# The first stage of a two-block transformer kernel: modulation as one half and two quarters, four projection chunks held in PSUM, and memory slabs moved into the half

## The chip, the cores and the metric

The kernel runs on one core of one Trainium2 chip. The metric is the device time of one execution in microseconds (us). The engines are TensorE (PE in the profile; PEld is its weight load), VectorE (DVE), ScalarE (ACT), GpSimd (POOL, unused here) and SyncE (SP), which issues nearly all transfers.

## The reference, cut to what matters

Two transformer blocks run one after the other over 256 tokens of width 2048. Only the start of the first block is touched, and a part of the second that depends on an input of its own:

```python
ada = jax.nn.silu(c) @ w_ada[l] + b_ada[l]            # 2048 -> 6 x 2048
shift_m, scale_m, gate_m, shift_f, scale_f, gate_f = split(ada)
h = rms_norm(x, g_pre_mix[l]) * (1.0 + scale_m) + shift_m
z = h @ w_in[l]                                       # 2048 -> 3920
...
k, v = jnp.split(mem_n @ wkv, 2, axis=-1)             # second block: 256 memory rows, 2048 -> 2 x 512
```

`z` is then split into the inputs of a latent attention (MLA) and a gated linear attention (GLA). All weights are float32.

## The kernel before, in words

**Slabs.** Every weight passes through four raw buffers of 128 x 2048 float32 (`raw`, 1 MiB each), which SP fills in one order written out by hand. A slab is 1024 KB, or less where a chunk is narrower. SP may issue slab n when slab n-4 is done (`slab_done`, L434). There are two kinds:

- A *linear* slab feeds matmuls. ScalarE rounds it into `wh` (`hi`, L631), VectorE makes the rest `wl = raw - wh` (`lo`, L1964), which frees the raw buffer. TensorE then runs, for two row blocks and four k-tiles, three matmuls each, hi x hi, hi x lo and lo x hi (L1283 to L1285): 24 matmuls a slab (`slab_mm`). There are two `wh`/`wl` buffers; `hi` of a slab waits until the slab two before it is used (`slab_used`).
- A *modulation* slab (w_ada) is multiplied by silu(c) and added up by VectorE alone, in ACC, JUNK or ACC2, which frees the buffer.

Every engine walks the slabs in the same order, with its own program. `skip` and `st.next(False)` pass a slab that another engine handles.

**First stage.** x is normalised, turned by TensorE and copied to XS by ScalarE. Then ScalarE takes the statistics of the memory and the sines of the rotary angles, and only after those walks on through its slabs. The shift and scale of the modulation are made in four quarters of 512 columns. A quarter is 8 slabs (`ada_part`: 4 row tiles x 512 columns for shift or scale). VectorE adds a slab up in four 128x512 steps (L2165; the first ones L2157). TensorE sums over partitions with small matmuls (`mod_parts`, L1356, 32 instructions), VectorE makes shift and gain (`mod_part`), then ScalarE and VectorE make four k-tiles of the modulated h (`h_hi`, L732; `h_gained`, L2190; `h_lo`). Such a quarter of h lets one quarter of the rows of w_in be used. `ZCH` lists nine chunks of columns of w_in with widths 400, 512, 512, 320, 320, 416, 416, 512, 512; a chunk takes four slabs, one for each quarter of h, and two PSUM banks (one per row block). Three chunks (ZK = 3) are held in banks 0 to 5, and after each quarter of h three w_in slabs are used. The eight slabs of w_xkv (memory keys and values, banks 6 and 7) lie between them, and most of the next quarter's modulation slabs (`AHEAD`) are placed ahead of the w_in slabs. The order is 8 modulation slabs with 1 memory slab; then for q = 0, 1, 2: memory, 2 modulation, w_in, 1 modulation, w_in, 2 modulation, w_in, 1 modulation, memory, 2 modulation; then memory and three w_in. That makes 52 slabs: 32 modulation, 8 memory, 12 w_in.

**Loop.** The other six chunks follow, 24 slabs (ZR = 24), with GLA's work between them (`a_turn`, `gate`, `cumulated`, ... on TensorE, the gate functions on ScalarE, the scans on VectorE). One full row tile of 8 KB per partition of the gate modulation goes with most slabs (`ADA_SHIFT`: 16 of them, into ACC), and 7 of the next (`ADA_NEXT`, into ACC2) with the last ones. ACC must have been zeroed (`acc_zero`, L2004) before SP loads a bias row into it (L444); SP does so in order, after the second slab of the loop. `ADA_FIRST` = 7 is how many rows of the second sum are made in the loop. The rest come later: two with w_uk and w_uv, one before and six within MLA's head loop (VectorE, L1985), where the number is KT - ADA_FIRST - 3.

## Time and profile before

| | |
|---|---|
| median of 3 runs | 2699.1 us (2698.87 to 2699.74) |
| the profiled execution | 2705.51 us, span 2703.7 us |
| TensorE busy | 2602.7 us (96% of the span) |
| VectorE busy | 1668.6 us (62%) |
| ScalarE busy | 1151.0 us (43%) |
| mean granted TensorE clock | 0.981 |
| read from HBM | 561.69 MB, 210 GB/s over the span |

A busy TensorE is not one at its peak: ends of matmuls are modelled, so a pipelined matmul shows 390 ns where the next starts 230 ns later. A wait in brackets behind an instruction is idle time of its engine, with what ended it. "x24" is a count of merged instructions. Idle time of an engine that is not the bottleneck costs nothing by itself.

### The profile page before, as it was taken

The numbers are of one execution on the slowest core, as the hardware profiler recorded it, in microseconds if no ns is written. First come the engines' busy times: TensorE is split into PE (matmuls) and PEld (weight loads), VectorE is DVE, ScalarE is ACT, GpSimd is POOL, SyncE is SP. The second block draws the span as 40 slices with busy tenths as digits, with TensorE's granted clock in tenths as the row PEclk, the third lists the DMA queues.
The fourth block names the chain that finished last, engine by engine and source line by source line (L and its number), as shares of the span: only waits on it lengthen the run. The fifth ranks groups of instructions, "written<-read, shape, count | busy, mean of one in ns | idle before, by whom it ended". The sixth has DMA issues, their size and how long they took to land.

```text
span 2703.7 us, 30651 instructions
## 1 busy us (share of the span) xinstructions
PE 2602.7 (96%) x12149; PEld 2158.3 (80%) x12149; DVE 1668.6 (62%) x1700; ACT 1151.0 (43%) x1217; POOL 0.2 (0%) x4
## 2 busy tenths in 40 slices
PE   5899999899999999999999999999899999999998
PEld 4778778788887888887988888787688888888886
DVE  7878788856665555557446665655555555555556
ACT  5244544443333333335445455444653333333333
POOL 0000000000000000000000000000000000000000
PEclk8999999899999999999999999999999999999999
...
GB/s 330 360 262 324 330 220 324 243 252 253 254 253 209 190 192 191 186 186 157 239 172 140 150 147 152 171 202 153 143 187 186 186 189 191 193 188 186 186 187 139
DMA packets 268139, 568.20 MB, mean 210 GB/s; under 512 B 9857, under 2 KB 46591, under 8 KB 258704
## 3 DMA queue, kind: packets, MB, share of 16 engines
...
q8 instruction: 61, 1.00, 0.2%
q14 instruction: 28, 0.23, 0.0%
HBM read 561.69 MB, written 5.24 MB: 210 GB/s over the span
## 4 chain that ended last, share of the span: by engine, by line
PE 80%; DVE 5%; ACT 3%; issue 2%; DMA 1%; DVEq 0%; ACTq 0%
PE bank L1283 25%; PE bank L1285 24%; PE bank L1284 24%; ACT wh L631 2%; DVE wl L1964 1%; DVE ROWB L1964 1%; DVE ACC L1985 1%; DMA raw<-in_w_out 1%; PE bank L1252 1%; PE bank L1816 1%; PE bank L1645 1%; PE bank L1764 1%; PE bank L1799 0%; DVE X L2118 0%; DMA raw<-in_w_uq 0%
## 5 line engine op out<-in xcount | busy, mean ns | idle before, releaser
L1964 DVE TENSOR_TENSOR wl<-raw,wh 128x2048 fp32r<-128x2048 f32 (+4 forms) x434 | 975.6, 2248 | 875.6 <-ACT wh L631 875.1
L631 ACT ACTIVATE wh<-raw 128x2048 fp32r<-128x2048 f32 (+4 forms) x434 | 816.4, 1881 | 1317.9 <-PE bank L1285 1209.8
L1283 PE MATMUL bank<-wh,XTh 128*128 128x512 f32 (+4 forms) x2680 | 1044.5, 390 | 21.9 <-DVE wl L1964 15.9
L1285 PE MATMUL bank<-wh,XTl 128*128 128x512 f32 (+4 forms) x2680 | 1032.5, 385 | 0.0
L1284 PE MATMUL bank<-wl,XTh 128*128 128x512 f32 (+4 forms) x2680 | 1031.6, 385 | 0.0
L1283 PEld LDWEIGHTS bank<-wh,XTh 128*128 128x128 f32 x2680 | 506.1, 189 | 126.8 <-issue 18.3
L1285 PEld LDWEIGHTS bank<-wh,XTl 128*128 128x128 f32 x2680 | 505.5, 189 | 94.4
L1284 PEld LDWEIGHTS bank<-wl,XTh 128*128 128x128 f32 x2680 | 506.2, 189 | 91.1 <-issue 0.5
L1283 PE MATMUL bank<-wh,HTh 128*128 128x512 f32 x640 | 251.1, 392 | 3.0 <-DVE ROWB L1964 3.0
L1285 PE MATMUL bank<-wh,HTl 128*128 128x512 f32 x640 | 249.2, 389 | 0.0
L1284 PE MATMUL bank<-wl,HTh 128*128 128x512 f32 x640 | 249.1, 389 | 0.0
L1283 PEld LDWEIGHTS bank<-wh,HTh 128*128 128x128 f32 x640 | 120.1, 188 | 34.7 <-issue 10.5
L1285 PEld LDWEIGHTS bank<-wh,HTl 128*128 128x128 f32 x640 | 120.1, 188 | 25.1
L1284 PEld LDWEIGHTS bank<-wl,HTh 128*128 128x128 f32 x640 | 120.2, 188 | 24.4
L1964 DVE TENSOR_TENSOR ROWB<-ROWB,bank 128x512 f32<-128x512 f32 x176 | 112.7, 682 | 8.8 <-PE bank L1285 7.2
L1985 DVE SCALAR_TENSOR_TENSOR ACC<-raw,cT,ACC 128x2048 f32<-128x2048 f32 x46 | 108.0, 2349 | 2.5
L1981 DVE SCALAR_TENSOR_TENSOR ACC<-raw,cT,ACC 128x2048 f32<-128x2048 f32 x16 | 37.6, 2350 | 1.8 <-DVE wl L1964 1.2
L2165 DVE SCALAR_TENSOR_TENSOR JUNK<-raw,cT,JUNK 128x512 f32<-128x512 f32 x56 | 38.1, 747 | 0.0
L2165 DVE SCALAR_TENSOR_TENSOR ACC<-raw,cT,ACC 128x512 f32<-128x512 f32 x56 | 37.9, 745 | 0.0
L624 ACT ACTIVATE XTh<-bank,vT 128x256 fp32r<-128x256 f32 x54 | 21.5, 474 | 28.8 <-PE bank L1252 21.7
L1061 ACT ACTIVATE Z<-bank,nstat 128x512 f32<-128x512 f32 (+1 forms) x24 | 16.2, 674 | 41.3 <-PE bank L1285 41.2
L1283 PE MATMUL bank<-wh,MTh 128*128 128x512 f32 x64 | 28.6, 446 | 2.8 <-DVE wl L1964 1.1
...
## 6 DMA issues: line engine op xcount, KB each, us to landing
raw<-in_w_ada SPq DMA_DIRECT2D x96, 1024.0 KB, 6.3
raw<-in_w_in SPq DMA_DIRECT2D x48, 1024.0 KB, 5.2
raw<-in_w_ffn_gate SPq DMA_DIRECT2D x44, 1024.0 KB, 5.2
raw<-in_w_ffn_up SPq DMA_DIRECT2D x44, 1024.0 KB, 5.2
raw<-in_w_ffn_down SPq DMA_DIRECT2D x44, 1024.0 KB, 5.0
raw<-in_w_gate SPq DMA_DIRECT2D x44, 1024.0 KB, 5.2
raw<-in_w_up SPq DMA_DIRECT2D x44, 1024.0 KB, 5.1
raw<-in_w_down SPq DMA_DIRECT2D x44, 1024.0 KB, 5.0
```

What stands on the lines that cost most here:

```text
L631: act.activation(wh[:, st.lin % 2, 0:width], raw[:, st.raw % 4, 0:width], ACT.Copy).then_inc(hi_made, 1)
L1252: mm = pe.transpose(PB[turn_bank(name, b)][:, SEQ * k + P * r:SEQ * k + P * r + P], src(r, 2 * b + k), ident)
L1283: pe.matmul(out_, hi_t[:, k, rows], w[0][:, q, :], start=first and q == 0, stop=False)
L1284: pe.matmul(out_, hi_t[:, k, rows], w[1][:, q, :], start=False, stop=False)
L1285: mm = pe.matmul(out_, lo_t[:, k, rows], w[0][:, q, :], start=False, stop=last and q == n - 1)
L1645: mm = pe.transpose(PB[4 + b][:, SEQ * q + P * r:SEQ * q + P * r + P], HROW[:, r, P * (2 * b + q):P * (2 * b + q) + P], ident)
L1764: pe.matmul(PB[2 + u % 2][:, 0:2 * nk].rearrange("p (b n) -> p b n", b=2), QT(i, par, r), KT2(g, nk), start=True, stop=True).then_inc(S("n ...
L1816: pe.matmul(PB[7][:, HD * b:HD * b + HD], pT[:, u % 2, P * blk_:P * blk_ + P], Z2[:, k, c0:c0 + HD], start=k == 0, stop=k == r)
L1964: return dve.tensor_tensor(out_, a, b, op)
L1981: ins = dve.scalar_tensor_tensor(acc[:, :], w, cT[:, bass.ds(k0 + k, 1)], acc[:, :], ALU.mult, ALU.add)
L1985: ins = dve.scalar_tensor_tensor(acc[:, :], w, cT[:, k:k + 1], acc[:, :], ALU.mult, ALU.add)
L2165: ins = dve.scalar_tensor_tensor(part, w, c, part, ALU.mult, ALU.add)
```

## The change

- The modulation of the first 1024 columns is made at once (`ada_half`: 16 slabs, one row tile each, 1024 columns of shift and 1024 of scale, one 128x2048 step into ACC), the rest in two quarters (`ada_quarter`: 8 slabs each, two row tiles, two transfers of 512 KB on one semaphore, two 128x1024 steps into JUNK or ACC).
- Three stages with an order made by `interleaved`: (0) two modulation slabs, then memory slab and two modulation slabs by turns, the eighth memory slab last; (1) w_in slab and one quarter slab by turns, for four chunks (ZK = 4) and the two quarters of h that the half gives, the last w_in slab after the last two quarter slabs; (2) w_in slab and two quarter slabs by turns, the fourth w_in slab last, behind four.
- The fourth use of the four chunks is moved into the loop as its first four slabs (`z_slab`). The loop still has 24 slabs: these four, and five chunks.
- Memory keys are summed in banks 4 and 5, values in 6 and 7; the key transposes use banks 2 and 3. All eight banks then hold the four chunks. Banks of the later chunks, of the gate and of the cq and ckv turns are swapped to suit, and TensorE waits for the last chunk's copies ahead of w_uq.
- GLA's steps are placed one slab later in the loop, the statistics of the latents one group earlier. `acc_zero` comes after the last quarter of h. ADA_FIRST is 6 instead of 7.

The diff, cut to its core. `mod_part` becomes `mod_made`, with the same three steps on 8 columns for the half:

```diff
@@ -83,14 +83,33 @@
 FN_ADA = KT // 4
-ZK = 3
-ZR = 4 * (ZN - ZK)
-AHEAD = ((0, 1), (2,), (3, 4))
-ADA_SHIFT = (1, 2, 3) + tuple(range(5, 18))
-ADA_NEXT = {ZR - 6: 1, ZR - 5: 2, ZR - 4: 1, ZR - 3: 1, ZR - 2: 1, ZR - 1: 1}
+ZK = 4
+ZR = 4 * (ZN - ZK) + 4
+ADA_SHIFT = (2, 3) + tuple(range(5, 19))
+ADA_NEXT = {ZR - 5: 2, ZR - 4: 1, ZR - 3: 1, ZR - 2: 1, ZR - 1: 1}
 next_row = {n: sum(ADA_NEXT[m] for m in ADA_NEXT if m < n) for n in ADA_NEXT}
 ADA_FIRST = sum(ADA_NEXT.values())
 XKV = [(i // 4, i % 4) for i in range(8)]
+def interleaved(slabs, rows, first, each):
+    steps = [("ada", k) for k in range(first)]
+    k = first
+    for i in range(slabs - 1):
+        steps.append(("slab", i))
+        steps += [("ada", k + m) for m in range(each)]
+        k += each
+    return steps + [("ada", m) for m in range(k, rows)] + [("slab", slabs - 1)]
+STAGES = [interleaved(8, 16, 2, 2), interleaved(8, 8, 0, 1), interleaved(4, 8, 0, 2)]
+MOD_READY = (4, 4, 6, 8)
+def z_slab(n):
+    return (n, 3) if n < 4 else (3 + n // 4, n % 4)
 BUCKETS, MAXD = 32, 2048
 REL_W = SEQ + P
...
+    def landed(self, transfers=1):
+        return self.plus(16 * (self.raw // 4 + self.more[self.raw % 4] + transfers), 4 * self.praw)
+    def next(self, linear=True, transfers=1):
+        self.more[self.raw % 4] += transfers - 1
...
-        return 2 + (TURN0[name] + b) % 2
+        return (TURN0[name] + b) % 2
...
+        mod_at = PB[1][:, 496:512]
         def z_banks(c):
-            return (2 * c, 2 * c + 1) if c < ZK else (2 * (c % 2), 2 * (c % 2) + 1)
+            return (2 * c, 2 * c + 1) if c < ZK else (2 - 2 * (c % 2), 3 - 2 * (c % 2))
...
-            def ada_part(v, q, s):
-                slab(W["w_ada"][:, 4 * s:4 * s + 4, v * D + 512 * q:v * D + 512 * q + 512], (4, 512), False)
+            def ada_half(k):
+                rows = W["w_ada"][:, k, 0:2 * D].rearrange("p (v n) -> p v n", v=2)
+                slab(rows[:, :, 0:1024], (2, 1024), False)
+            def ada_quarter(q, k):
+                rows = [W["w_ada"][:, 2 * k + t, 0:2 * D].rearrange("p (v n) -> p v n", v=2)[:, :, 512 * q:512 * q + 512]
+                        for t in range(2)]
+                sp.wait_ge(slab_done, st.raws(-3))
+                for t in range(2):
+                    dst = raw[:, st.raw % 4, 1024 * t:1024 * t + 1024].rearrange("p (v n) -> p v n", v=2)
+                    sp.dma_start(dst, rows[t]).then_inc(landed[st.raw % 4], 16)
+                st.next(False, 2)
...
-            for v in range(2):
-                for s in range(4):
-                    ada_part(v, 0, s)
-                if v == 0:
-                    xkv(0)
-            for q in range(4):
-                xkv(2 * q + 1)
-                for c in range(ZK):
-                    if q < 3:
-                        for s in AHEAD[c]:
-                            ada_part(s // 4, q + 1, s % 4)
-                    cols("w_in", q, *ZCH[c])
-                if q < 3:
-                    ada_part(1, q + 1, 1)
-                    xkv(2 * q + 2)
-                    for s in range(2, 4):
-                        ada_part(1, q + 1, s)
-                if q == 1:
+            for what, i in STAGES[0]:
+                ada_half(i) if what == "ada" else xkv(i)
+            for what, i in STAGES[1]:
+                ada_quarter(2, i) if what == "ada" else cols("w_in", i % 2, *ZCH[i // 2])
+                if (what, i) == ("slab", 3):
                     sp.wait_ge(S("rel_row"), 1)
                     sp.wait_ge(S("angle"), 1)
...
+            for what, i in STAGES[2]:
+                ada_quarter(3, i) if what == "ada" else cols("w_in", 2, *ZCH[i])
...
-                cols("w_in", n % 4, *ZCH[ZK + n // 4])
+                cols("w_in", z_slab(n)[1], *ZCH[z_slab(n)[0]])
...
+            for what, i in STAGES[0][3:]:
+                if what == "ada":
+                    skip()
+                    continue
                 hi()
...
+            h_hi(0)
+            for what, i in STAGES[1]:
+                if what == "ada":
+                    st.next(False, 2)
+                    continue
+                hi(4 * ZCH[i // 2][1])
+                if i == 0:
+                    h_hi(1)
+                if i == 1:
+                    act.wait_ge(slab_used, 8)
+                    for r in range(RB):
+                        act.activation(xv[:, r, :], PB[6 + r][:, :], ACT.Copy, scale=mem_scale(r)).then_inc(chunk_out, 1)
+            h_hi(2)
+            for what, i in STAGES[2]:
+                if what == "ada":
+                    st.next(False, 2)
+                else:
+                    hi(4 * ZCH[i][1])
+            h_hi(3)
...
-                if n < 2:
-                    z_evac(n + 1, 19 + n)
-                if n % 4 == 1 and n > 4:
-                    z_evac(ZK + n // 4 - 1, st.lin - 2)
+                hi(4 * ZCH[z_slab(n)[0]][1])
+                if 2 <= n < 6:
+                    z_evac(n - 2, st.lin - 2)
+                elif n % 4 == 1 and n > 6:
+                    z_evac(2 + n // 4, st.lin - 2)
...
+                if n == 18:
                     gla_squares(0)
                     gla_squares(1)
-                if n == 18:
+                    for name, width in (("cq", QR), ("ckv", KVR)):
+                        norm_stats(name, latent(name), width, junk=JUNK2[:, 512:1024])
+                if n == 19:
                     gla_squares(2)
                     gla_squares(3)
-                    for name, width in (("cq", QR), ("ckv", KVR)):
-                        norm_stats(name, latent(name), width, junk=JUNK2[:, 512:1024])
...
+            def mod_half():
+                pe.wait_ge(slab_done, st.raws())
+                for v in range(2):
+                    for k in range(8):
+                        c0 = 1024 * v + P * k
+                        mm = pe.matmul(mod_at[:, 8 * v + k:8 * v + k + 1], ACC[:, c0:c0 + P], ones[:, 0:1], start=True, stop=True,
+                                       skip_group_check=True)
+                    mm.then_inc(S("mod_sum"), 2)
+            def mod_quarter(q):
                 pe.wait_ge(slab_done, st.raws())
                 for v in range(2):
                     for k in range(4):
+                        o = mod_at[:, 8 * (q - 2) + 4 * v + k:8 * (q - 2) + 4 * v + k + 1]
                         for par in range(2):
+                            c0 = 1024 * par + 512 * v + P * k
+                            mm = pe.matmul(o, (JUNK, ACC)[q - 2][:, c0:c0 + P], ones[:, 0:1], start=False, stop=par == 1,
                                            skip_group_check=True)
                     mm.then_inc(S("mod_sum"), 1)
...
+                slab_mm((4 + 2 * c, 5 + 2 * c), ALL[4 * s:4 * s + 4], 512, s == 0, s == 3, lhs=(MTh, MTl))
             pe.wait_ge(S("rel_row"), 1)
             pe.wait_ge(S("vec_out"), 2)
+            for what, i in STAGES[0]:
...
+                if i == 7:
+                    mod_half()
+                xkv(i)
+                if i == 5:
                     pe.wait_ge(chunk_out, RB)
...
+            for what, i in STAGES[1]:
+                if what == "ada":
                     st.next(False)
+                    continue
+                c, s = i // 2, i % 2
+                if i == 2:
+                    pe.wait_ge(S("xk_out"), 2)
+                if i == 6:
+                    pe.wait_ge(chunk_out, RB * 2)
+                if i == 7:
+                    mod_quarter(2)
+                pe.wait_ge(S("x_lo"), 2 * s + 2)
+                slab_mm(z_banks(c), ALL[4 * s:4 * s + 4], ZCH[c][1], s == 0, False)
+            pe.wait_ge(S("x_lo"), 6)
+            for what, i in STAGES[2]:
+                if what == "ada":
+                    st.next(False)
+                    continue
+                if i == 3:
+                    mod_quarter(3)
+                slab_mm(z_banks(i), ALL[8:12], ZCH[i][1], False, False)
+            pe.wait_ge(S("x_lo"), 8)
...
             for n in range(ZR):
-                c = ZK + n // 4
-                if n % 4 == 0:
-                    pe.wait_ge(chunk_out, RB * {ZK: 4, ZK + 1: 5}.get(c, CHUNK0["zin"] + c - 1))
-                slab_mm(z_banks(c), ALL[4 * (n % 4):4 * (n % 4) + 4], ZCH[c][1], n % 4 == 0, n % 4 == 3)
+                c, s = z_slab(n)
+                if s == 0:
+                    pe.wait_ge(chunk_out, RB * (CHUNK0["zin"] + c - 1))
+                slab_mm(z_banks(c), ALL[4 * s:4 * s + 4], ZCH[c][1], s == 0, s == 3)
                 for _ in range((n in ADA_SHIFT) + ADA_NEXT.get(n, 0)):
                     st.next(False)
-                if n == 0:
...
             turned_ready("ckv")
+            pe.wait_ge(chunk_out, RB * CHUNK0["uq"])
...
+            def ada_half(k):
                 dve.wait_ge(landed[st.raw % 4], st.landed())
+                if st.raw:
+                    dve.wait_ge(slab_done, st.raws())
+                w, c = raw[:, st.raw % 4, :], cT[:, k:k + 1]
+                if k == 0:
+                    ins = dve.tensor_scalar(ACC[:, :], w, c, None, ALU.mult)
+                else:
+                    ins = dve.scalar_tensor_tensor(ACC[:, :], w, c, ACC[:, :], ALU.mult, ALU.add)
+                ins.then_inc(slab_done, 1)
+                st.next(False)
+            def ada_quarter(q, k):
+                dve.wait_ge(landed[st.raw % 4], st.landed(2))
+                dve.wait_ge(slab_done, st.raws())
+                for t in range(2):
+                    acc = (JUNK, ACC)[q - 2][:, 1024 * t:1024 * t + 1024]
+                    w, c = raw[:, st.raw % 4, 1024 * t:1024 * t + 1024], cT[:, 2 * k + t:2 * k + t + 1]
+                    if k == 0:
+                        ins = dve.tensor_scalar(acc, w, c, None, ALU.mult)
                     else:
+                        ins = dve.scalar_tensor_tensor(acc, w, c, acc, ALU.mult, ALU.add)
+                ins.then_inc(slab_done, 1)
+                st.next(False, 2)
+            def mod_made(q, n, at):
...
+            for what, i in STAGES[0]:
+                ada_half(i) if what == "ada" else lo()
+                if (what, i) == ("ada", 1):
                     norm_row2("x")
...
+                if (what, i) == ("slab", 2):
+                    norm_inv("mem")
+                    dve.wait_ge(S("squared"), 2 * RB)
+            mod_made(0, 8, mod_at)
+            h_gained(0)
+            h_lo(0)
+            for what, i in STAGES[1]:
+                ada_quarter(2, i) if what == "ada" else lo(4 * ZCH[i // 2][1])
+                if (what, i) == ("slab", 0):
+                    h_gained(1)
+                    h_lo(1)
+            mod_made(2, 4, mod_at[:, 0:8])
+            h_gained(2)
+            h_lo(2)
+            for what, i in STAGES[2]:
+                ada_quarter(3, i) if what == "ada" else lo(4 * ZCH[i][1])
+            mod_made(3, 4, mod_at[:, 8:16])
+            h_gained(3)
+            h_lo(3)
+            acc_zero()
```

## Rows read from the trace of the kernel before

**Rows 1.** Busy time by window, whole core; the first line names the columns.

```profile
core 0: us, PE busy (x) PEld busy (x) DVE busy (x) ACT busy (x) POOL busy (x), PEclk, DMA share, GB/s
50.00:160.00 110.00, 96.71 (x438) 80.86 (x438) 96.89 (x131) 34.74 (x31) 0.00 (x0) 0.91 0.98 352
80.00:100.00 20.00, 18.41 (x89) 14.89 (x87) 18.36 (x28) 6.04 (x8) 0.00 (x0) 0.91 1.04 376
48.50:58.80 10.30, 9.67 (x39) 9.09 (x40) 8.33 (x15) 2.29 (x2) 0.00 (x0) 0.50 1.04 374
168.00:174.80 6.80, 6.80 (x23) 5.83 (x23) 3.60 (x10) 3.50 (x5) 0.00 (x0) 0.50 0.58 212
160.00:193.50 33.50, 33.48 (x153) 28.64 (x154) 20.23 (x23) 13.44 (x15) 0.00 (x0) 0.90 0.62 210
193.50:333.10 139.60, 134.90 (x711) 114.92 (x709) 112.05 (x82) 69.05 (x92) 0.00 (x0) 1.00 0.91 322
```

**Rows 2.** Waits of the DMA queue (SP), 0 to 210 us: total, times, longest.

```profile
SPq L434 <- DVE wl L1964: 76.7, 24, 7.8
...
SPq L444 <- DVE ACC L2004: 8.1, 1, 8.1
```

**Rows 3.** TensorE in order of time: start us, us, line, operation.

```profile
49.13 6.99 PE L1356 MATMUL bank<-CON,ACC 128*128 128x1 f32 x32 [3.48 <-DVE ACC L2165]
...
126.31 3.63 PE L1356 MATMUL bank<-CON,ACC 128*128 128x1 f32 x32
...
193.26 0.39 PE L1285 MATMUL bank<-wh,XTl 128*128 128x512 f32 x1
193.49 0.30 PE L1283 MATMUL bank<-wh,XTh 128*128 128x320 f32 x1
...
332.96 0.39 PE L1285 MATMUL bank<-wh,XTl 128*128 128x512 f32 x1
```

**Rows 4.** VectorE in order of time, four modulation rows, `lo`, two rows.

```profile
31.42 5.38 DVE L2165 SCALAR_TENSOR_TENSOR ACC<-raw,cT,ACC 128x512 f32<-128x512 f32 x8
36.72 2.29 DVE L1964 TENSOR_TENSOR wl<-raw,wh 128x2048 fp32r<-128x2048 f32 x1
...
302.41 4.81 DVE L1985 SCALAR_TENSOR_TENSOR ACC<-raw,cT,ACC 128x2048 f32<-128x2048 f32 x2
```

**Rows 5.** ScalarE in order of time at the start.

```profile
32.50 1.91 ACT L631 ACTIVATE wh<-raw 128x2048 fp32r<-128x2048 f32 x1 [0.27 <-DMA raw<-in_w_xkv]
...
38.51 1.09 ACT L624 ACTIVATE XS<-bank 128x512 f32<-128x512 f32 x2 [0.20 <-PE bank L1252]
...
45.17 0.31 ACT L624 ACTIVATE cs<-ang 128x128 f32<-128x128 f32 x1
48.97 1.91 ACT L631 ACTIVATE wh<-raw 128x2048 fp32r<-128x2048 f32 x1 [3.48 <-DMA raw<-in_w_xkv]
```

**Rows 6.** The DMA queue in order of time: issues of slabs 4 and 12.

```profile
27.49 0.37 SPq L434 DMA_DIRECT2D raw<-in_w_xkv  x1
...
49.11 0.37 SPq L434 DMA_DIRECT2D raw<-in_w_in  x1
```

**Rows 7.** VectorE in order of time at the last quarter.

```profile
170.28 0.16 DVE L1964 TENSOR_TENSOR modA<-bank,bT 128x4 f32<-128x4 f32 x1 [2.39 <-PE bank L1356]
...
174.28 1.82 DVE L1964 TENSOR_TENSOR wl<-raw,wh 128x1600 fp32r<-128x1600 f32 x1 [0.66 <-ACT wh L631]
...
182.78 1.76 DVE L2004 MEMSET ACC<- 128x2048 f32 x1 [0.38 <-issue]
```

**Rows 8.** The chain that ended last, in attention.

```profile
388.34 2.26 DVE ACC L1985
...
392.43 2.26 DVE ACC L1985
```

**Rows 9.** DMA issues, 0 to 300 us: count, KB, us to landing.

```profile
raw<-in_w_ada SPq DMA_DIRECT2D x51, 1024.0 KB, 6.8
...
raw<-in_w_in SPq DMA_DIRECT2D x8, 640.0 KB, 5.4
```

197 lines of the change are left out of this document (54 added, 143 removed).

## The prediction

> **What bounds the kernel now.** The median of the runs shown is 2699.1 us; the profiled execution took 2705.5 us with a span of 2703.7 us, so it lies 6.4 us (0.24%) above that median. The sum below is a difference between two points of the trace, and I add it to the median. About 0.2% (5.4 us) is what a measurement of this kernel can tell from no change.
>
> I read the windows first, then the waits of the DMA queue, then the instructions of each engine in order of time. The windows [rows 1] cut the part that the change touches in two. Up to 160 us transfers and VectorE are both nearly full: the DMA engines 98% busy at 352 GB/s, VectorE 96.9 of 110 us. TensorE has gaps there. From 160 to 193.5 us TensorE is busy throughout (33.5 of 33.5 us) while the transfers fall to 210 GB/s, and in the loop over the rest of the projection, 193.5 to 333.1 us, it is busy 134.9 of 139.6 us. So the first part is set by how fast slabs pass four buffers, and from 160 us on by TensorE's own work. The DMA queue's waits say the same [rows 2]: every slab issue waits for VectorE to free a buffer (76.7 us behind the subtraction `lo` alone), and 8.1 us go by where the bias row waits for ACC to be zeroed. A change in the first part is worth what it moves the point at which TensorE has the loop's first slab (193.49 us before, [rows 3]), corrected for the work then left.
>
> **The change part by part.**
>
> *VectorE's work on the modulation.* Before, a slab of w_ada is four 128x512 steps, eight in 5.38 us, so 2.7 us a slab [rows 4]; 32 slabs with the cheaper first steps are about 82 us. After, 16 slabs are one 128x2048 step. Two such with their waits took 4.81 us, 2.4 each [rows 4]. The other 16 are two 128x1024 steps, a shape that no row has; between 0.67 (the 512 step) and 2.4 us lies, by width, 1.2 us, so 2.5 a slab with its wait. Together 75 us: 7 us less. This pays only where VectorE holds up the transfers.
>
> *The start: a loss.* Slab order is now rows 0, 1, memory 0, rows 2, 3, memory 1. ScalarE makes `hi` of memory slab 1 only after its last XS copy (39.60 us) and the statistics of the memory, which end with the sine at 45.48 us [rows 5]. So `hi` ends at 45.5 + 1.9 = 47.4 and `lo` (2.3 us, [rows 4]) at 49.7. VectorE has nothing else in its order after rows 2 and 3, done at about 41 us. Before, this stretch was covered: four modulation slabs stood ahead of that `lo`, and ScalarE waited for the transfer, not the reverse [rows 5]. With slab 5 done at 49.7, slab 9 is issued then; before, slab 12 was issued at 49.1 [rows 6]. Three slabs are lost.
>
> *Transfers from there.* Slab 9 starts on an idle queue, which takes 5.0 us (27.49 to 32.50, [rows 5, 6]), so it lands at 54.7. To slab 51, the end of the three stages, there remain 25 modulation slabs, 5 of memory and 12 of projection, 40.2 MiB. At the 376 GB/s of the best stretch a MiB takes 2.79 us, at the 352 GB/s of the whole part 2.98 [rows 1]. I take 2.87, 115.4 us in all, since VectorE now hinders less: slab 51 lands at 170.1 if nothing stops the queue. The small GLA loads in this part cost about 2 us, as far as they hold up one slab: 172.
>
> *First handover (half to first quarter).* Every row of the half must be in before anything is projected. Let memory slab 7 land at L. Slab 6 landed three slabs earlier, its `lo` ends at L-4.0, its matmuls (24 at 0.23 us, [rows 3], 5.5 us) at L+1.5. The column sums, 32 instructions as before, take 3.63 us [rows 3], to L+5.1. From the sums' end to the end of `lo` of the next projection slab was 5.8 us (170.28 to 176.10, [rows 7]), so that slab's buffer is free at L+10.9 and the next transfer lands at L+15.9. The four buffers held 3.56 MiB, which at full speed would have let it land at L+12.7. Lost: 3.2 us, and 1.6 more on the next buffer, which also waits for quarter 1's own steps.
>
> *Second handover.* TensorE runs some 4.5 us behind the last row (its slabs need 5.5 us each against 5.6 for the pair of transfers); sums and the same chain end 13.9 us after that row has landed, against buffers worth 12.3 us plus 2.8. The restart costs 5.0, so 3.8 us are lost. Slab 51: 172 + 4.8 + 3.8 = 180.6; the last modulation row, one 0.63 MiB slab earlier, 178.8.
>
> *Third handover, the exposed one.* VectorE's step 2.5 us, sums 3.63, then the 5.8 us chain with the zeroing of ACC (1.76 us, [rows 7]) now inside it ahead of `lo`: 178.8 + 2.5 + 3.6 + 5.8 + 1.8 = 192.5 us for the loop's first slab. TensorE has one slab of width 320 (3.5 us) under it and idles for about 4 us. Before, four whole slabs were queued at this point, and the same chain was hidden by memory slab 7 and cost nothing. The bias row's 8.1 us [rows 2] go, but the DMA queue still waits for ACC with three slabs prefetched, so TensorE gains nothing there.
>
> *The loop.* Before, 24 slabs with 9984 columns-times-slabs took 139.6 us [rows 1]. After, the first four are the last quarter of four chunks: 10448. The 464 more, times 24 matmuls at 0.23 us per 512, are 5.0 us. First slab at 192.5 against 193.5, end at 337.1 against 333.1 [rows 3]: 4.0 us late.
>
> *One modulation row moved behind.* ADA_FIRST falls from 7 to 6, so attention holds seven rows instead of six. The chain there runs through them, 2.26 us each [rows 8], with no cover: +2.3 us. The loop loses one row and gains nothing, since TensorE bounds it.
>
> *Costed at nothing.* The second DMA instruction of a quarter slab: SP spends 0.37 us on an issue [rows 6] and one falls due every 2.8 us. The new wait ahead of w_uq: the last chunk's copies stand on ScalarE ahead of ckv's, for which TensorE waits anyway; behind it are only the uq slabs. Latent statistics one group earlier: ScalarE has `hi` two slabs ahead, cover 5.5 us a slab. Bank moves: work and instruction counts stay.
>
> Sum: 4.0 + 2.3 = 6.3, so 2699.1 + 6.4 = 2705.5 us.
>
> A split transfer could cost more. In the rows, transfers overlap: 1024 KB land in 6.8 us after issue, 640 KB in 5.4 [rows 9], while the queue moves one MiB every 2.8 us, so a fixed part of about 2 us is hidden. The Trainium skill, DMA: Bandwidth & Descriptors, section Bandwidth, asks for at least 1 MiB per DMA. By that rule the 512 KB halves would be a loss of their own (rival 4).
>
> **Rivals.**
>
> 1. *Faster: VectorE was the bound.* It is busy 88% of the part to 160 us, and SP always waits for it. If the handovers are covered better than I reckon (TensorE less behind, buffers refilled in time), the losses of 4.8 and 3.8 us vanish and the start costs perhaps one slab (2.8 us) less: 11.4 us back, so 2694; with the better transfer rate (40.2 x 0.08 = 3.2 us) 2691. Against: with 98% DMA share there is little for VectorE to give back.
> 2. *No difference.* Half of that, about 5 us: 2700.
> 3. *Slower by the clock, decided where TensorE idles between slabs.* The granted clock was 0.50, that is 1.2 GHz, from 48.5 to 58.8 us, after TensorE had waited for VectorE, and again from 168.0 to 174.8, during and after the last column sums [rows 1]; sums that ran at the low level took 6.99 us against 3.63 [rows 3]. In the half stage TensorE has 5.5 us of work per 8.6 us, in the last quarter 5.5 per 8.4. If the slow level holds at both exposed handovers, each sum costs 3.4 us more and the slab with it up to 3.5: 7 us, 2712. It decides only if it falls within the chain to the loop's first slab; earlier it is hidden by transfers. The Trainium skill, TensorE: Matmul & The Clock Gate, section "HAM oscillation — how this bites in real kernels", says that short compute between waits for transfers leaves the array slow tile after tile; the trace agrees in that the slow stretches follow the sums and the waits.
> 4. *Slower by split transfers.* If two 512 KB pieces went one after the other, each with its fixed part, a slab would take some 2 us more: sixteen give 32 us, 2737. The overlap in [rows 9] speaks against it.
> 5. That the change does not do what it says can be left aside: orders and counts are written out.
>
> **How the numbers follow.** Forecast (handovers lose what I sum, 2701 to 2709): 0.50. Rival 1: 0.19. Rival 2: 0.18. Rival 3: 0.11. Rival 4: 0.02. The forecast sits 1 us beyond the 0.2% bound, so a third of it falls within: faster 0.19, within 0.2% 0.36, slower 0.45. Bounds of the unknown costs: transfer pace +4.4/-3.2 us, the two 1024 steps 0.3 us a slab only where exposed. The range takes in rival 1 at 2691 and most of rival 3: 2690 to 2714.
>
> **What would show it.** Right: slab 5's `lo` near 49.7 us; VectorE idle from 41 to 47; gaps of some 5 us in the transfers at about 106 and 155 us; TensorE idle just ahead of the loop, whose first slab comes near 192.5; end of the loop near 337; attention with seven rows. Wrong: the loop's first slab before 186, or `hi` of memory slab 1 not waiting for the statistics; then the forecast falls to rival 1. Slab pace of 4 us in the quarters would mean rival 4.

## The result, and the profile after

The changed kernel took 2715.7 us (median of 11 runs, 2706.08 to 2724.24). The kernel before, run beside it, took 2701.0 us (11 runs, 2698.87 to 2709.19). The ratio, which is formed from all runs and not from the two medians, is 1.0047, with a 95% interval of 1.0037 to 1.0057: slower by 12.7 us, where 6.4 were forecast (the medians alone are 14.7 us apart). Carried over to the 2699.1 us of the forecast this is 2711.8 us, inside the range of 2690 to 2714; the median itself lies 1.7 us above the range.

| | before | after |
|---|---|---|
| profiled execution | 2705.51 us, span 2703.7 | 2717.23 us, span 2715.5 |
| TensorE busy | 2602.7 us | 2607.8 us |
| VectorE busy | 1668.6 us | 1661.7 us |
| ScalarE busy | 1151.0 us | 1149.8 us |
| mean granted TensorE clock | 0.981 | 0.977 |

VectorE has 6.9 us less to do, as forecast (7), and it is of no use. The time is lost in five places. The windows of the changed kernel come first, with the columns of [rows 1].

```profile
core 0: us, PE busy (x) PEld busy (x) DVE busy (x) ACT busy (x) POOL busy (x), PEclk, DMA share, GB/s
28.00:50.00 22.00, 14.20 (x61) 12.22 (x62) 12.94 (x7) 18.09 (x21) 0.00 (x0) 0.73 0.68 240
50.00:160.00 110.00, 98.74 (x455) 83.22 (x454) 91.17 (x74) 35.64 (x33) 0.00 (x0) 0.92 0.95 337
160.00:193.35 33.35, 24.47 (x102) 21.23 (x102) 24.53 (x26) 8.60 (x8) 0.00 (x0) 0.80 0.77 277
193.35:336.70 143.35, 139.73 (x710) 117.73 (x710) 111.96 (x82) 70.01 (x95) 0.00 (x0) 1.00 0.89 313
```

The start's window in the kernel before, not shown yet:

```profile
28.00:50.00 22.00, 13.26 (x60) 11.71 (x61) 21.12 (x32) 16.86 (x22) 0.00 (x0) 0.73 0.96 333
```

Against these and [rows 1]: the middle is nearly the same (337 GB/s where it was 352), but the start moves only 240 GB/s instead of 333 and leaves VectorE busy for 12.9 us instead of 21.1, and the last 33 us ahead of the loop have TensorE busy for 24.5 us, where it had been busy all the time. The loop is longer by 3.5 us (143.35 us to the end of its last instruction, where it was 139.86).

**The start.** ScalarE's and then VectorE's instructions in order of time (start us, us, engine, line, operation, idle time before it and what ended it):

```profile
39.62 1.92 ACT L644 ACTIVATE JUNK<-MEM 128x2048 f32<-128x2048 f32 x1
...
43.26 0.31 ACT L644 ACTIVATE cs<-ang 128x128 f32<-128x128 f32 x1
43.48 1.89 ACT L651 ACTIVATE wh<-raw 128x2048 fp32r<-128x2048 f32 x1
```

```profile
34.93 4.81 DVE L2207 SCALAR_TENSOR_TENSOR ACC<-raw,cT,ACC 128x2048 f32<-128x2048 f32 x2
45.41 2.29 DVE L2012 TENSOR_TENSOR wl<-raw,wh 128x2048 fp32r<-128x2048 f32 x1 [5.67 <-ACT wh L651]
```

`hi` of memory slab 1 starts right behind the sine, with no wait for a transfer, and VectorE stands idle for 5.67 us until it is there. The DMA queue issues nothing between 39.8 and 47.7 us, since the four buffers are full. This is the first loss of the forecast. It comes 2 us earlier in absolute time than reckoned, for the most part because ScalarE reached its statistics of x 1.4 us earlier in this execution (22.74 us, where it was 24.12 before and 23.75 in a second execution of the change).

**The first two handovers.** The forecast had gaps in the transfers at about 106 and 155 us. They are there, each some 3 us early, as the start was 2 us early (same columns):

```profile
101.50:105.00 3.50, 3.50 (x17) 2.95 (x16) 3.37 (x6) 2.32 (x6) 0.00 (x0) 1.00 0.22 45
151.00:154.50 3.50, 3.40 (x18) 3.16 (x18) 3.24 (x3) 1.50 (x2) 0.00 (x0) 0.87 0.18 36
```

In each of these 3.5 us the transfer engines are busy for a fifth of the time. That is 2.7 and 2.9 us without transfers, where 3.2 (and 1.6 more on the next buffer) and 3.8 were forecast.

**The handover into the loop.** TensorE in order of time; its waits in the last quarter of the modulation, the loop's first slab, its last instruction:

```profile
168.78 0.62 PE L1310 MATMUL bank<-wh,XTh 128*128 128x512 f32 x1 [3.80 <-DVE wl L2012]
...
179.12 6.89 PE L1393 MATMUL bank<-CON,ACC 128*128 128x1 f32 x32 [2.99 <-DVE ACC L2221]
...
193.35 0.42 PE L1310 MATMUL bank<-wh,XTh 128*128 128x400 f32 x1 [2.10 <-DVE wl L2012]
...
336.31 0.39 PE L1312 MATMUL bank<-wh,XTl 128*128 128x512 f32 x1
```

The loop's first slab comes at 193.35 (forecast 192.5; before 193.49, [rows 3]), its end at 336.7 (forecast 337.1; before 333.35, the end of the last instruction of [rows 3]). The sums took 6.89 us, at the lower clock level, where [rows 3] has both 3.63 and 6.99.

**Attention.** VectorE with the last two rows of modulation 3, each behind a head of attention, and the start of the first head without one:

```profile
401.91 2.34 DVE L2033 SCALAR_TENSOR_TENSOR ACC<-raw,cT,ACC 128x2048 f32<-128x2048 f32 x1
404.17 0.55 DVE L2012 TENSOR_TENSOR prob<-bank,CON 128x384 f32<-128x384 f32 x1
404.75 0.61 DVE L2419 TENSOR_REDUCE mst<-prob 128x1 f32<-128x128 f32 x2
405.28 0.15 DVE L2424 RECIPROCAL mst<-mst 128x2 f32<-128x2 f32 x1
405.47 0.61 DVE L2426 TENSOR_SCALAR Z<-bank,mst 128x128 f32<-128x128 f32 x2
406.00 2.34 DVE L2033 SCALAR_TENSOR_TENSOR ACC<-raw,cT,ACC 128x2048 f32<-128x2048 f32 x1
408.26 0.55 DVE L2012 TENSOR_TENSOR prob<-bank,CON 128x384 f32<-128x384 f32 x1
```

VectorE is without a gap here, so a head costs 4.09 us with a row (404.17 to 408.26). In the kernel before the same head had none and took 1.82 us (394.61 to 396.43): 2.27 us more, where 2.26 were forecast.

**The clock.** The windows of attention's heads and of what follows them, same columns:

```profile
372.00:400.00 28.00, 27.70 (x118) 19.01 (x117) 19.06 (x29) 11.67 (x39) 0.00 (x0) 0.70 0.61 212
400.00:426.00 26.00, 22.09 (x113) 19.23 (x112) 17.42 (x34) 11.08 (x25) 0.00 (x0) 0.74 0.48 163
```

Before, the same two windows had 1.00 and 0.87. In this execution the granted clock was at its lower level (0.50, which is 1.2 GHz) from 373.8 to 390.9 us and from 411.4 to 425.0. The first slab of w_out, the weight behind attention, starts at 425.2 instead of 410.1 us, 15.1 us late: 3.9 were there when attention began, 2.3 are the row, and the rest of nearly 9 falls on the stretches at the lower clock. The profiled execution as a whole is 11.8 us longer, so 3.3 us of the delay come back before the end.

So a profile alone can't say what the change costs: part of the 12.7 us is structure (work and waits that the change moves), part is a clock that differs between two executions of the same kernel. The experiments separate them.

### The profile page after: what moved, and what is told of

It is laid out like the page before. It is cut to its first block, busy times and chain, and to the rows that moved or that the text cites. A ratio compares the mean times of both kernels' runs of the same rounds, so it can differ in the third digit from the quotient of the medians.

```text
span 2715.5 us, 30584 instructions
## 1 busy us (share of the span) xinstructions
PE 2607.8 (96%) x12117; PEld 2161.3 (80%) x12117; DVE 1661.7 (61%) x1617; ACT 1149.8 (42%) x1217; POOL 0.2 (0%) x4
## 4 chain that ended last, share of the span: by engine, by line
PE 82%; DVE 7%; ACT 5%; DMA 3%; issue 2%; SPq 0%; DVEq 0%; ACTq 0%
PE bank L1310 25%; PE bank L1312 25%; PE bank L1311 25%; ACT wh L651 3%; DVE wl L2012 2%; DMA raw<-in_w_in 1%; DVE ROWB L2012 1%; PE bank L1279 1%; DMA raw<-in_w_out 1%; PE bank L1864 1%; PE bank L1693 1%; DVE ACC L2033 1%; DMA raw<-in_w_xkv 1%; ACT JUNK L644 1%; DVE ACC L2207 1%
## 5 line engine op out<-in xcount | busy, mean ns | idle before, releaser
L2012 DVE TENSOR_TENSOR wl<-raw,wh 128x2048 fp32r<-128x2048 f32 (+3 forms) x434 | 975.5, 2248 | 877.1 <-ACT wh L651 876.5
L651 ACT ACTIVATE wh<-raw 128x2048 fp32r<-128x2048 f32 (+3 forms) x434 | 816.4, 1881 | 1336.2 <-PE bank L1312 1218.7
L2012 DVE TENSOR_TENSOR ROWB<-ROWB,bank 128x512 f32<-128x512 f32 x176 | 112.7, 682 | 8.8 <-PE bank L1312 7.2
L2033 DVE SCALAR_TENSOR_TENSOR ACC<-raw,cT,ACC 128x2048 f32<-128x2048 f32 x46 | 108.0, 2348 | 2.4
L2029 DVE SCALAR_TENSOR_TENSOR ACC<-raw,cT,ACC 128x2048 f32<-128x2048 f32 x16 | 37.6, 2350 | 1.8 <-DVE wl L2012 0.8
L2207 DVE SCALAR_TENSOR_TENSOR ACC<-raw,cT,ACC 128x2048 f32<-128x2048 f32 x15 | 35.3, 2351 | 1.5
L2166 DVE SCALAR_TENSOR_TENSOR X<-ROWB,nstat,X 128x512 f32<-128x512 f32 x40 | 27.6, 747 | 0.2
```

The costliest lines, as they stand in the source:

```text
L651: act.activation(wh[:, st.lin % 2, 0:width], raw[:, st.raw % 4, 0:width], ACT.Copy).then_inc(hi_made, 1)
L2012: return dve.tensor_tensor(out_, a, b, op)
L2029: ins = dve.scalar_tensor_tensor(acc[:, :], w, cT[:, bass.ds(k0 + k, 1)], acc[:, :], ALU.mult, ALU.add)
L2033: ins = dve.scalar_tensor_tensor(acc[:, :], w, cT[:, k:k + 1], acc[:, :], ALU.mult, ALU.add)
L2166: dve.scalar_tensor_tensor(x, y, nstat[:, j, 2, r:r + 1], x, ALU.mult, ALU.add).then_inc(S("x_added"), 1)
L2207: ins = dve.scalar_tensor_tensor(ACC[:, :], w, c, ACC[:, :], ALU.mult, ALU.add)
```

## The experiments

Eleven experiments follow: ten new kernels, and the change once more (8). Each run comes with its mean granted clock. Over the runs of the change, of the experiments and of the kernel before beside them (179 in all) one line fits within each kernel: 1.49 us (plus or minus 0.07) more for each 0.001 of mean clock less, and a scatter of 1.7 us around it. Read at one clock (0.982, that of the kernel before), two kernels compare with an error of 0.5 to 0.9 us. In the table "at one clock" is that reading, and "mean clock" is over the runs of the kernel. A sitting is a group of runs taken together with the kernel before: experiments 1 to 4, then 5 to 8, then 9 to 11, each on another chip. The kernel before reads 2702.2 to 2703.1 us on these three, so a comparison across sittings can be off by up to that much more. The 11 runs of the kernel before that stand beside the first result have no clock on record and are not in the table.

| kernel | median us (runs) | ratio, 95% interval | mean clock | at one clock |
|---|---|---|---|---|
| before, three sittings | 2702.4 (14), 2701.1 (29), 2703.2 (29) | 1 | 0.9822, 0.9822, 0.9820 | 2703.1, 2702.2, 2702.7 |
| the change | 2715.7 (11) | 1.0047 (1.0037 to 1.0057) | 0.9785 | 2710.1 |
| the change again | 2713.3 (5) | 1.0037 (1.0020 to 1.0055) | 0.9804 | 2710.1 |
| 1 seventh row back in the loop | 2707.7 (7) | 1.0024 (1.0013 to 1.0035) | 0.9813 | 2707.0 |
| 2 statistics later | 2706.9 (8) | 1.0027 (1.0016 to 1.0038) | 0.9800 | 2705.8 |
| 3 two slabs behind | 2718.2 (5) | 1.0062 (1.0048 to 1.0076) | 0.9784 | 2713.1 |
| 4 four steps | 2714.7 (5) | 1.0046 (1.0032 to 1.0059) | 0.9804 | 2711.7 |
| 5 both mended | 2704.2 (12) | 1.0007 (0.9997 to 1.0016) | 0.9816 | 2703.5 |
| 6 before, seventh row in attention | 2706.1 (12) | 1.0016 (1.0006 to 1.0026) | 0.9815 | 2705.6 |
| 7 halves split too | 2711.3 (9) | 1.0038 (1.0025 to 1.0051) | 0.9804 | 2709.0 |
| 9 both mended, eight rows in the loop | 2706.5 (12) | 1.0013 (1.0003 to 1.0022) | 0.9809 | 2703.7 |
| 10 before, eight rows in the loop | 2701.4 (12) | 0.9995 (0.9987 to 1.0004) | 0.9825 | 2702.6 |
| 11 as 9, nine rows | 2704.1 (10) | 1.0011 (0.9998 to 1.0023) | 0.9825 | 2706.5 |

At one clock the change costs 2710.1 - 2702.6 = 7.5 us, where 6.4 were forecast. The remaining 4.5 us go with its clock: 0.9791 over its 16 runs against 0.9821, 0.0030 at 1.49 us for each 0.001. This split is as good as the slope. The runs of the kernel before alone give 1.30 (plus or minus 0.12), those of the change alone 1.88 (plus or minus 0.24), which makes the clock's part 3.9 or 5.7 us and the structural part 8.1 or 6.3. It is also a correlation over runs: no experiment set the clock.

### 1. The seventh row back into the loop

```
-ADA_NEXT = {ZR - 5: 2, ZR - 4: 1, ZR - 3: 1, ZR - 2: 1, ZR - 1: 1}
+ADA_NEXT = {ZR - 6: 1, ZR - 5: 2, ZR - 4: 1, ZR - 3: 1, ZR - 2: 1, ZR - 1: 1}
```

> The changed kernel with the seventh row of the second sum put back into the loop (ADA_FIRST 7, six rows within the head loop). Theory: the head loop's chain loses one row of 2.26 us, the loop is bound by TensorE and takes it in for nothing, so 2.3 us less than the changed kernel: ratio to the kernel before 1.0039 instead of 1.0047, loop end still at 336.7 us (within 1). Rival: the loop has no room for it, loop end 2.3 us later and nothing won, ratio 1.0047. Rival on the clock: if the slow stretch in the head loop (373.8 to 390.9 us in the changed kernel's trace) belongs to the change, it is there again; if it comes and goes from run to run, the trace may lack it.

Measured: ratio 1.0024. Against the change that is 6 us, more than the row's 2.3; at one clock it is 3.1 us (error 0.8), and the other 3 are a mean clock of 0.9813 instead of 0.9791. The loop takes the row nearly for nothing: from its first slab (191.58) to its end (335.43) it lasts 143.9 us, with six rows 143.4, and this execution had a stretch at the lower clock in the loop (234.0 to 239.9 us) that the other lacked. The windows of attention in this kernel:

```profile
372.00:400.00 28.00, 25.47 (x142) 17.68 (x142) 25.68 (x45) 13.76 (x49) 0.00 (x0) 1.00 0.77 274
400.00:426.00 26.00, 24.53 (x138) 21.40 (x137) 19.25 (x24) 12.63 (x18) 0.00 (x0) 0.87 0.57 201
```

The heads run at the full clock here, and so they do in the traces of experiments 3 to 10, the change run again (8) among them.

### 2. The memory statistics behind `hi` of memory slab 1

```
             for b in range(TURN_N["x"]):
...
-            norm_stats("mem", lambda r: MEM[:, r, :], D)
-            act.wait_ge(S("angle"), 1)
-            f(cs[:, :, :, :], ang[:, :, :, :], ACT.Sin, "sines")
...
                 hi()
+                if i == 1:
+                    norm_stats("mem", lambda r: MEM[:, r, :], D)
+                    act.wait_ge(S("angle"), 1)
+                    f(cs[:, :, :, :], ang[:, :, :, :], ACT.Sin, "sines")
```

> The changed kernel with ScalarE's statistics of the memory and the sines placed behind hi of memory slab 1 instead of ahead of it. Theory: lo of memory slab 1 ends at about 42 us instead of 47.7, the next stall (slab 2) is covered by rows 4 and 5, so transfers run 5 us ahead and the loop's first slab comes at about 188.5 instead of 193.35; 5 us less in all, ratio 1.0029. Rival: VectorE or the handovers take the slack up again: loop's first slab at 192 or later, ratio 1.0045 or more.

VectorE's first instructions in order of time, and the start's window:

```profile
35.02 4.81 DVE L2208 SCALAR_TENSOR_TENSOR ACC<-raw,cT,ACC 128x2048 f32<-128x2048 f32 x2
39.74 2.28 DVE L2013 TENSOR_TENSOR wl<-raw,wh 128x2048 fp32r<-128x2048 f32 x1
42.13 4.81 DVE L2208 SCALAR_TENSOR_TENSOR ACC<-raw,cT,ACC 128x2048 f32<-128x2048 f32 x2
```

```profile
28.00:50.00 22.00, 17.52 (x80) 14.96 (x80) 16.64 (x9) 18.19 (x21) 0.00 (x0) 0.82 0.86 312
```

The gap of 5.67 us is gone, the transfers run at 312 GB/s instead of 240, and the loop's first slab starts at 189.31 us, 4.0 earlier. The time follows: 4.3 us less at one clock (error 0.7). The loss at the start is real, and the delay goes through all three stages to the end.

### 3. Two projection slabs held behind the last rows of each stage

```
+TAIL = 2
...
-    for i in range(slabs - 1):
+    for i in range(slabs - TAIL):
...
-    return steps + [("ada", m) for m in range(k, rows)] + [("slab", slabs - 1)]
+    return steps + [("ada", m) for m in range(k, rows)] + [("slab", i) for i in range(slabs - TAIL, slabs)]
```

> The changed kernel with two linear slabs instead of one behind the last modulation row of every stage. Theory: TensorE has 9 to 11 us of work under each chain of sums, shift and gain, rounding, and the buffers are refilled in time: no idle time ahead of the loop's first slab (was 2.1 us, and 3.0 and 3.8 us ahead of it in the last quarter), loop's first slab at 186 to 188, 6 us less in all, ratio 1.0025. Rival: the handovers cost nothing and only the order changes: loop's first slab at 193, ratio 1.0047.

A miss. Meant to hide the handovers, it made the kernel 3.0 us slower at one clock (error 0.9). TensorE's waits in the last quarter:

```profile
164.78 0.50 PE L1313 MATMUL bank<-wh,XTh 128*128 128x512 f32 x1 [1.61 <-DVE wl L2015]
...
181.07 6.99 PE L1396 MATMUL bank<-CON,ACC 128*128 128x1 f32 x32 [10.57 <-DVE ACC L2224]
```

The cover works: the two held slabs run from 188 to 199 us and TensorE has no wait ahead of the loop. But that work was taken from the time in which TensorE waits for the rows, where it cost nothing: 10.57 us of idle time stand there now, against 3.80 and 2.99 in the change, and the loop's first slab comes at 199.0, 5.7 us later. The rows' arrival is what ends last. The held work lasts 11 us and the handover that it covers some 7 (7.3 us from the end of the sums to the loop's first slab in the change), so the difference is added length. The same was done at all three handovers, and what it did at each was not tried alone.

### 4. The modulation in four 128x512 steps again

```
-                    ins = dve.scalar_tensor_tensor(ACC[:, :], w, c, ACC[:, :], ALU.mult, ALU.add)
+                for t in range(4):
+                    part = ACC[:, 512 * t:512 * t + 512]
...
-                for t in range(2):
-                    acc = (JUNK, ACC)[q - 2][:, 1024 * t:1024 * t + 1024]
+                for t in range(4):
+                    acc = (JUNK, ACC)[q - 2][:, 512 * t:512 * t + 512]
```

> The changed kernel with every modulation slab added up in four 128x512 steps again, order and transfers unchanged. That is 0.3 us more VectorE work a slab, 10 us in all. Theory: VectorE is not what holds up the first part any more, so only the steps within the three chains and the start show: loop's first slab 1 to 2 us later, ratio 1.0050 to 1.0055. Rival (VectorE is the bound): most of the 10 us shows, loop's first slab at 201 or later, ratio 1.0075 or more.

Ratio 1.0046, 1.6 us slower than the change at one clock (error 0.9). VectorE's extra 9 us (1670.9 us busy instead of 1661.7) cost 1 or 2: it does not bound this part. In its trace the loop's first slab came at 198.7, 5.3 us later than in the change, with the sums slow again (6.99 us), and w_out's first slab at 423.9 all the same, 1.3 earlier, with the heads at the full clock. So a single trace can overstate such a loss. Its groups up to 195 us, first in the change, then here (total us, mean ns):

```profile
L2207 DVE SCALAR_TENSOR_TENSOR ACC<-raw,cT,ACC 128x2048 f32<-128x2048 f32 x15 | 35.3, 2351 | 1.5
...
L2221 DVE SCALAR_TENSOR_TENSOR ACC<-raw,cT,ACC 128x1024 f32<-128x1024 f32 x14 | 17.4, 1282 | 0.7
```

```profile
L2209 DVE SCALAR_TENSOR_TENSOR ACC<-raw,cT,ACC 128x512 f32<-128x512 f32 x60 | 41.1, 746 | 1.5
L2223 DVE SCALAR_TENSOR_TENSOR JUNK<-raw,cT,JUNK 128x512 f32<-128x512 f32 x28 | 19.2, 747 | 0.7
```

The 128x1024 step, which no row of before showed, took 1.28 us (estimated at 1.2), and a quarter slab 2.5 as said.

### 5 and 6. Both mended, and the seventh row alone in the kernel before

Experiment 5 has the edits of 1 and 2 together. Experiment 6 is the kernel before with `ADA_NEXT = {ZR - 5: 2, ...}`, one row fewer in its loop.

> The changed kernel with both mended places at once: seven rows of modulation 3 in the loop (so six in attention, as before the change), and the memory statistics and the sine behind hi of memory slab 1. Alone they came to ratios of 1.0024 and 1.0027 where the change had 1.0047, so 2.3 and 2.0 thousandths were won, 6.2 and 5.4 us. Theory (two separate places, a start loss and a row in attention with what it does to the clock there): the gains add, ratio 1.0004, within 0.9992 and 1.0016; loop's first slab near 189.3, first w_out slab near 409, slow stretch about the sums of modulation 3 of 7 us. Rival A (both gains are mostly the clock's chance from kernel to kernel, and only the 2.3 us of the row and some 3 of the start are real): they add only in part, ratio 1.002 to 1.003. Rival B (the start's lead is swallowed as soon as attention is freed): ratio 1.0024, as with the row alone.

> The kernel before with one thing of the change alone: six rows of modulation 3 in the loop and the seventh in attention. Theory (the row costs its load and its step, 2.3 us, in the chain at the end of attention, and the longer idle of TensorE there stretches the slow clock about the sums of modulation 3 from 6.8 us to 13 or 14): ratio 1.0018 to 1.0026, 5 to 7 us; the sums at 403 and taking 6.8 us; first w_out slab at 415 to 417 where before it was at 410. Rival A (the row alone, no clock): ratio 1.0009, sums taking 4.2 us, w_out at 412.4. Rival B (the row was no loss in the kernel before, since its loop had spare time at the end that this frees: the loop ends 2.3 us earlier): ratio 1.000.

The gains add: experiment 5 lies at 1.0007, its interval holding 1, and at one clock 6.6 us under the change, where 1 and 2 gave 3.1 and 4.3 alone. 0.9 us (error 0.6) are left over the kernel before for the handovers and the longer loop together (1.3 us against the kernel before of the same sitting). Experiment 6 puts the row at 3.0 us at one clock (error 0.6), and experiment 1 puts it at 3.1 from the other side, against 2.27 by the trace. Both lie above it by little more than their errors. The loop did not gain by losing the row: 139.5 us where it was 139.9. My theory that the row also stretches the slow clock behind it failed here. The windows of experiment 6:

```profile
372.00:400.00 28.00, 22.68 (x130) 16.04 (x131) 26.79 (x46) 13.07 (x49) 0.00 (x0) 1.00 0.80 278
400.00:426.00 26.00, 25.68 (x140) 22.81 (x139) 19.73 (x22) 12.26 (x13) 0.00 (x0) 0.87 0.64 230
```

0.87 as before, not the 0.74 of the change, and w_out began at 411.1 where 415 to 417 were expected. Its mean clock, 0.9815, is hardly below 0.9821.

### 7. Twice as many split transfers

```
-                slab(rows[:, :, 0:1024], (2, 1024), False)
+                for v in range(2):
+                    sp.dma_start(raw[:, st.raw % 4, 1024 * v:1024 * v + 1024], rows[:, v, 0:1024]).then_inc(landed[st.raw % 4], 16)
```

> The changed kernel with the suspected cost of a second DMA instruction doubled: each of the 16 slabs of the modulation's first half is loaded by two transfers too (one for each 1024 columns of shift and of scale), as each of the 16 quarter slabs is. Theory (the second transfer costs nothing, the bytes alone count): within 0.1% of the change itself, ratio 1.0037 to 1.0057, loop's first slab within 1 us of 193.4. Rival (split transfers move at a lower rate or cost an issue on the path; the forecast's rival took 1.26 us for each split slab): 16 times 1.26 is 20 us more, ratio 1.012, loop's first slab near 213.

No cost: 1.0038, at one clock 1.1 us under the change (error 0.7), the loop's first slab at 193.33 (193.35). The expectation names 1.26 us a slab for the forecast's rival, which had said some 2 us; both, 20 or 32 us for sixteen slabs, are ruled out. One of its nine runs took 13406 us; it is in no mean here. The issues of w_ada up to 300 us, of the change and of this kernel (count, KB, us from issue to landing):

```profile
raw<-in_w_ada SPq DMA_DIRECT2D x34, 1024.0 KB, 6.7
raw<-in_w_ada SPq DMA_DIRECT2D x32, 512.0 KB, 6.4
```

```profile
raw<-in_w_ada SPq DMA_DIRECT2D x64, 512.0 KB, 6.0
raw<-in_w_ada SPq DMA_DIRECT2D x18, 1024.0 KB, 6.5
```

512 KB take nearly as long to land as 1024. That fits waiting behind other transfers in flight, though a fixed part of each transfer was not told apart from it. The Trainium skill, DMA: Bandwidth & Descriptors, section Bandwidth, asks for at least 1 MiB a transfer. Here, with several slabs in flight, halves of that size cost nothing: 16 slabs more were split, and the time at one clock was 1.1 us less (error 0.7).

### 8. The change once more

> The changed kernel once more, for a second trace: which of its slow stretches of TensorE's clock come back. Theory: the stretch about the sums of modulation 3 (411 to 425) is there again, 13 or 14 us long, since the seventh row makes it; the stretch in the first heads of attention (374 to 391) was chance and may be gone, and then the first w_out slab is at 419 to 422 instead of 425.2. Rival (the change fixes the clock at the first heads as well): both stretches are there at the same places. The time, by either: ratio 1.0037 to 1.0057.

Windows of attention in this execution of the same kernel:

```profile
372.00:400.00 28.00, 25.02 (x141) 17.65 (x142) 23.64 (x38) 14.45 (x49) 0.00 (x0) 1.00 0.74 257
400.00:426.00 26.00, 22.18 (x105) 19.98 (x105) 16.94 (x30) 10.18 (x19) 0.00 (x0) 0.67 0.48 162
```

The slow heads are gone, and w_out begins at 421.2 instead of 425.2 us: that stretch belonged to the first execution. The stretch behind the heads is there again (403.9 to 420.9). Over all traces the second window (400 to 426 us) has a granted clock of 0.67 to 0.74 in five of the six traces with the new order and six rows in the loop (the change, its repeat, 2, 3, 4; in 7 it is 0.87), and 0.87 to 1.00 in every other trace. Where the clock drops is partly the kernel's and partly chance, and one trace can't tell which.

### 9, 10 and 11. More rows in the loop

Since the loop had taken the seventh row nearly for nothing, I tried an eighth (`ZR - 7: 1` added) in the mended version and in the kernel before, and a ninth (`ZR - 7: 2`).

> The changed kernel with the memory statistics and the sine moved back behind hi of memory slab 1, and with eight rows of modulation 3 in the loop, one more than before the change. Taken at one clock (all runs so far on a common line of 1.5 us for each 0.001 of mean granted clock), the seventh row cost 3.1 us in attention, and the loop took it up for nothing (loop's first slab to its end 143.4 us with six rows and with seven). Theory: the loop has room for an eighth as well, and attention gives its 3.1 us again: against the seven-row version's ratio of 1.0007, 0.9995, within 0.9985 and 1.0006; loop 143.4 us long, seventh to ninth slab positions unmoved. Rival (DMA in the loop is full: its busy share is 0.98 from 250 to 300 already, so 1 MB more takes 2.9 us there): the loop grows by 2.9 us and the ratio stays at 1.0004 to 1.0010.

> The kernel before with one row of modulation 3 more in the loop, eight instead of seven, and nothing of the change. Theory (a row in attention costs 3.1 us and one in the loop nothing): ratio 0.9989, within 0.998 and 0.9997; w_out's first slab at 407 where before it was at 410. Rival (the loop before has its transfers at 0.90 of their engines, the row's 2.9 us are hidden only in part, or the eighth row's place in attention is hidden behind ScalarE): ratio 0.9997 to 1.0005.

> As the version with eight rows in the loop, and a ninth beside the eighth, at the same loop slab. Theory (each row out of attention is worth 3.1 us until the loop's transfers are full): the loop takes the ninth only in part, ratio 0.9985 to 0.9997. Rival (the loop's transfers bound it, as the busy share of 0.98 from 250 to 300 says): it grows by 2.9 us for each of the two rows, ratio 1.0005 to 1.0015.

Misses for my theory: at one clock the eighth row gives 0.0 in the kernel before (error 0.6) and 0.2 us the other way in the mended one (error 0.7), and with the ninth it is 3 us slower. For the eighth row the loop is not why: in experiment 9 it lasts 144.0 us, within the 142.9 to 145.5 of the kernels with fewer rows. In experiment 10 it lasts 141.6 where it was 139.9, and 1.4 of these 1.7 us arise in one slab at about 230 us, where the clock dropped. With the ninth row the loop is why, at least in part: it lasts 149.9 us, and TensorE waits 2.63 us for VectorE's `wl` at 317.0, where the longest such wait late in any other loop is 1.17 (experiment 6). Its ratio, 1.0011, lies where the rival of its expectation had it. Where the eighth row's gain goes is seen in attention. VectorE in experiment 10, behind its last row:

```profile
394.06 0.17 DVE L2375 RECIPROCAL mst<-mst 128x2 f32<-128x2 f32 x1 [0.55 <-PE bank L1602]
...
395.95 0.56 DVE L1964 TENSOR_TENSOR prob<-bank,CON 128x384 f32<-128x384 f32 x1 [1.08 <-PE bank L1582]
...
399.58 0.17 DVE L2375 RECIPROCAL mst<-mst 128x2 f32<-128x2 f32 x1 [1.67 <-PE bank L1602]
```

Before, VectorE was full up to the last head's softmax, and then waited 0.59 and 1.02 us for TensorE; now it waits 0.55, 1.08 and 1.67. So 1.7 of the row's 2.3 us go over into waits for TensorE, for the scores and for the products with the values: the end of attention passes from VectorE's chain to TensorE's. Seven rows in the loop, the count of the kernel before, is the number from which one fewer costs a full row and one more gives nothing. No version beats both kernels: experiment 10 comes nearest, level with the kernel before.

## Why the prediction was right, and where it fell short

The direction was right and so were the places of the structural losses. The size was not: 12.7 us is twice the 6.4 forecast (the terms themselves add to 6.3), and the time fell within the range because the range had been drawn up to rival 3, the clock. In part that is luck, since the clock acted mostly at another place than that rival said.

- **VectorE's work, 7 us less, worth little:** right. 6.9 us less over the kernel; four steps again cost 1.6 us (experiment 4).
- **The start:** right in mechanism, and in the idle time: the forecast had VectorE idle from 41 to 47, it was from 39.7 to 45.4. The three slabs counted as lost were too many. Slab 12 was issued at 54.84 us, 5.7 later than before ([rows 6]), which is two slabs of 2.87 us. The later statistics won 4.3 us (experiment 2), somewhat more than half of the structural loss.
- **Transfers and handovers:** the sum, 192.5 us, was within 0.9 of the trace's 193.35, but by terms that offset each other. The sums of the last quarter began at 179.12 (forecast: rows landed at 178.8, step to 181.3), 2.2 us early, and took 6.89 us instead of 3.63, 3.3 too long. From their end to the loop's first slab went 7.3 us, of which 7.6 were forecast. With the start mended that slab came at 189.3 (experiment 2) and in another execution at 191.4 (experiment 5): a spread of 2 us, twice this term's error. The same spread lies in the starting point. The forecast took 193.49 from one execution; experiments 6 and 10, which have the kernel before's order up to there, have it at 190.8 and 191.1. The first two handovers cost the transfers 2.7 and 2.9 us, as said above. What they and the third cost in the final time has no price of its own: the one attempt to hide them (experiment 3) made other time exposed.
- **The bias row:** I let 8.1 us of the queue's wait go. It was 12.1 us in the trace after. As forecast, TensorE shows no wait for it: its first long wait in the loop (2.91 us, at 242.5) is for VectorE (Z, L2012).
- **The loop:** +5.0 forecast, +3.5 in these two traces, its end at 336.7 for 337.1. The traces with the new order and up to eight rows have loops of 142.9 to 145.5 us (mean 144.1), those with the order before 139.5 to 141.6 (mean 140.3, with experiments 6 and 10): 3.7 us more, part of it slow stretches. Mended at the other two places, the kernel keeps 0.9 us over the one before at one clock. That fits, as its loop also starts earlier: with the later statistics the first slab comes at 189.3, 189.3 and 191.4 us (experiments 2, 9 and 5), with the order before at 193.5, 190.8 and 191.1. The ends of the loop are 332.2, 333.3 and 336.9 against 333.4, 330.3 and 332.7. They spread by more than their means differ (2.0 us), so the term stands, and its size in the final time is known no better than to 1 or 2 us.
- **The row in attention:** right in mechanism and in its own time: 2.27 us in the trace, 3.1 and 3.0 by experiments 1 and 6, errors 0.8 and 0.6. That the loop gains nothing by losing it: right too (139.5 us for 139.9 in experiment 6). The forecast did not see that in the new order the row goes with a lower clock as well, as the last point says.
- **Costed at nothing** (second DMA instruction, the wait ahead of w_uq, bank moves): right as far as it was tried. Experiment 7 doubled the split transfers without cost, and w_uq's first slab starts 3.3 us behind the loop's last where it was 3.5. The bank moves and the earlier latent statistics were not tried alone.
- **The step that failed: the clock.** It stood as rival 3 at 0.11, with the forecast's own terms at full clock, and was to decide only within the chain to the loop's first slab. There it did fall, on the sums (6.89 us, behind waits of 3.80 and 2.99 us). But the larger part is elsewhere: the mean clock is 0.9791 instead of 0.9821 over all runs, some 4.5 of 12.0 us (3.9 to 5.7, by the slope taken). The structural part is 7.5 us (8.1 to 6.3) against 6.4; the term that was mis-sized is the clock's, set at zero. The Trainium skill, TensorE: Matmul & The Clock Gate, section "HAM oscillation — how this bites in real kernels", cited with that rival, has the array slow where short work alternates with waits. The trace agrees at the sums; how much it comes to over this kernel only the runs show.

Which part of the change lowers the clock can be read in part from all runs together. The kernels with the new order and six rows in the loop (the change, its repeat, 2, 3, 4 and 7; 42 runs) have a mean clock of 0.9796, those with seven or more (1, 5, 9 and 11; 41 runs) 0.9816: 0.0020 more, with an error of 0.0004. At 1.49 us for each 0.001 that is 3.0 us, so the row in attention goes with most of the lower clock. (Experiment 1, which has nothing but the row back, has 0.9813.) It does so only in the new order: with the order before, moving it lowered the clock by 0.0006, with an error of 0.0006 (experiment 6). Why the two orders differ here stays open.
